# Small fp32 matmuls of three stages regrouped by array tile, and a 16-block inverse packed into 32 columns

## Chip, cores, metric

One core of a Trainium2 chip. The metric is the device time of one execution in microseconds (us), the median of the runs shown. The profile is of one further execution.

## The reference, cut to what matters

The kernel runs two two-layer blocks over 512 tokens of width 1024. The change touches three stages, all in fp32 accuracy.

Memory cross attention, twice (4 heads of 256, 256 memory rows): `p = softmax(q @ k.T / 16)`, `o = p @ v`, `o @ wo`.

Gated linear attention (GLA), once, 4 heads, chunks of 64 tokens: `scores = tril(q_dec @ k_inv.T)`, `o = scores @ v + q_dec @ S`, with `S` updated from chunk to chunk by `k_end.T @ v`, then a norm per head.

The delta rule (RWKV7), once, 8 heads of 64. The reference solves `(I - A_ab) sol = [a_dec, A_ak v]` in chunks of 16; the kernel does the same recurrence in chunks of 64. It inverts the diagonal 16 x 16 blocks of the 64 x 64 lower triangle by the product `(I+A)(I+A^2)(I+A^4)(I+A^8)`, since A^16 is zero there, and brings in what lies off the blocks (`off`) by three further products.

## The kernel before, in words

Every matmul goes through one helper (L190), every ScalarE copy through L207, every VectorE two-operand operation through L213. A dense product splits both sides into a high and a low fp32r part and issues three matmuls; each stands as one row of the trace. A matmul on unsplit fp32 stands as two rows, each with a weight load of its own. Weights come from HBM in units of 256 columns (SP's queue), ScalarE makes the high part (`W.round`), VectorE the low part (`W.rest`), two units ahead. Engines run their own programs in order and wait on semaphores; PSUM has eight banks, which `ps.take` hands out in turn from a list.

**Cross attention** (`xattn`, L996). Per head: scores (L1040), softmax on ScalarE and VectorE, transposes (`turn`), ScalarE's copy of them (`turned`, L1182), and `output_of` (L1063): four fp32 matmuls of 128 x 128 by 512. Query projections and output rows stand between these, in an order written out by hand.

**GLA** (`gla`, L1935). `updates` (L1989) makes the 8 chunk products of two heads, 16 matmuls with 64 x 64 weights: first those on array rows 0 to 63, then those on 64 to 127. `part` does one head's scores (4 matmuls, 64 rows and 128 columns of the array), its output (4 full ones, then 7 from the states, 64 rows and 128 columns), or its norm's sum. `heads()` (L1967) places these parts between sixteen blocks of the memory projection (24 matmuls of 256 columns each), on TensorE, VectorE and ScalarE alike. Those blocks take turns on two banks that ScalarE's copy empties.

**Delta rule** (`rwkv`, L2270). Heads go in four pairs p. Two chains, one for p = 0 and 2, one for p = 1 and 3 and begun 13 rounds later, run in step: each round (`together`, L425) issues the next piece of the one, of the other, and a number of dense pieces from the list `PIECES` (L2312), each three matmuls of a projection or one block of the second memory projection. Per p a chain has 6 rounds of features, 11 of heads and 11 of tail; from one piece to the next of the same chain stand VectorE's masks and sums or ScalarE's copies. The heads' pieces on TensorE (`heads_tensor`, L2408), all with 64 x 64 weights: two Gram products AdT and Ad (`gram`, L2421, 16 matmuls each; first those that stay in their half of the array, then, after a semaphore, those that cross over); aak and arb likewise; Q2T, Q2 and z (`square`, L2434, 16 each); Q4T, Q4, Y1; Q8, Y2; ark with Y3 between its halves; M and MT; then X0 to X2 (`apply`, 128 columns); G and S; and in the tail QT and y. VectorE's part is `heads_vector` (L2658), ScalarE's `heads_scalar` (L2826).

## Time and profile before

| | us |
|---|---|
| median of 3 runs (lowest, highest) | 2987.49 (2987.06, 2989.36) |
| the profiled execution, its own time | 2989.32 |
| its span in the profile | 2987.5 |
| TensorE busy | 2942.3 |
| VectorE, ScalarE, GpSimd busy | 1854.6, 1345.3, 324.1 |

The span is what the trace covers; the execution's own time is 1.8 us longer. GLA lies at about 14 to 183 us, the delta rule at 183 to 505, the first cross attention at 509 to 601, the second at about 1172 to 1263. The trace counts a matmul as busy from its start to its modelled end, so busy times of overlapping matmuls are a union, and a window's (x) counts the rows that run in it, also those begun before.

### The profile page before, as it was taken

To read this page: it belongs to the slowest core of one execution; us is meant where nothing else is said; L and a number is where in the kernel's file an instruction comes from. 1 tells how busy PE (TensorE), PEld (TensorE's weight loads), DVE (VectorE), ACT (ScalarE), POOL (GpSimd) and SP (SyncE) were. 2 spreads that over 40 slices of the span, in tenths; PEclk is the share of its full clock that TensorE was granted. 3 is DMA by queue.
4 is the path that set the end of the run, shared out by engine and by line. 5 is a ranking of instruction groups with operands and counts; after the bars stand their busy time and mean duration, and the time that the engine had idled before them with its cause. 6 is when DMAs were issued, how large, how long until landed. Compare 5 with 4: busy or idle time off the path is not lost.

```text
span 2987.5 us, 43166 instructions
## 1 busy us (share of the span) xinstructions
PE 2942.3 (98%) x18348; PEld 2479.3 (83%) x18348; DVE 1854.6 (62%) x2299; ACT 1345.3 (45%) x1799; POOL 324.1 (11%) x296
## 2 busy tenths in 40 slices
PE   8999999999999999999999999999999999999999
PEld 7877778787888777787888876799988888889998
DVE  5554565367776866367776656766665554566665
ACT  5543444345444674344434447544443333344442
POOL 0010001010000111010000200142410000014240
PEclk9999999999999999999999999999999999999999
DMA  5340123223333223133332331233332222233331
GB/s 193 120 128 16 49 88 127 86 81 93 99 103 96 93 71 113 43 83 105 97 107 93 91 83 29 78 102 103 103 119 77 97 84 79 86 91 103 103 103 67
DMA packets 329120, 275.00 MB, mean 92 GB/s; under 512 B 28784, under 2 KB 286832, under 8 KB 328416
## 3 DMA queue, kind: packets, MB, share of 16 engines
q1 hardware_dynamic: 324560, 252.83, 28.5%
q0 software_dynamic: 4368, 19.41, 1.9%
q8 instruction: 144, 2.36, 0.3%
q14 instruction: 48, 0.39, 0.0%
HBM read 263.83 MB, written 8.39 MB: 91 GB/s over the span
## 4 chain that ended last, share of the span: by engine, by line
PE 88%; DVE 7%; ACT 4%; issue 1%; DMA 0%; DVEq 0%; SPq 0%; ACTq 0%
PE ps L190 87%; DVE arena L213 2%; ACT whi L207 2%; DVE wlo L213 1%; DVE split L213 1%; PE ps L193 1%; ACT arena L207 1%; ACT arena L204 1%; DVE arena L221 1%; ACT split L207 1%; DVE hT L213 0%; DVE xlo L221 0%; DVE sml L230 0%; DVE arena L224 0%; ACT L204 0%
## 5 line engine op out<-in xcount | busy, mean ns | idle before, releaser
L190 PE MATMUL ps<-split,whi 128*128 128x512 f32 (+2 forms) x3296 | 942.6, 364 | 7.0 <-ACT arena L207 4.6
L213 DVE TENSOR_TENSOR wlo<-wraw,whi 128x2048 fp32r<-128x2048 f32 (+3 forms) x262 | 562.2, 2147 | 431.9 <-ACT whi L207 431.1
L190 PE MATMUL ps<-xhi,whi 128*128 128x512 f32 (+1 forms) x1896 | 689.5, 369 | 7.4 <-DVE wlo L213 3.9
L190 PEld LDWEIGHTS ps<-split,whi 128*128 128x128 f32 (+1 forms) x3296 | 594.1, 188 | 121.0 <-issue 17.7
L190 PE MATMUL ps<-xhi,wlo 128*128 128x512 f32 (+1 forms) x1840 | 668.7, 363 | 0.0
L190 PE MATMUL ps<-xlo,whi 128*128 128x512 f32 (+2 forms) x1800 | 657.2, 365 | 0.0
L207 ACT ACTIVATE whi<-wraw 128x2048 fp32r<-128x2048 f32 (+3 forms) x262 | 457.8, 1749 | 351.1 <-PE ps L190 248.1
L190 PE MATMUL ps<-split,wlo 128*128 128x512 f32 (+2 forms) x1648 | 593.1, 360 | 0.0
L190 PEld LDWEIGHTS ps<-xhi,whi 128*128 128x128 f32 x1896 | 353.7, 188 | 75.9 <-issue 8.8
L207 ACT ACTIVATE arena<-ps 128x256 f32<-128x256 f32 (+1 forms) x429 | 204.9, 482 | 442.1 <-PE ps L190 365.4
L190 PEld LDWEIGHTS ps<-xhi,wlo 128*128 128x128 f32 x1840 | 346.6, 188 | 57.9 <-issue 4.3
L190 PEld LDWEIGHTS ps<-xlo,whi 128*128 128x128 f32 (+1 forms) x1800 | 338.6, 188 | 56.4
L190 PEld LDWEIGHTS ps<-split,wlo 128*128 128x128 f32 (+1 forms) x1648 | 310.7, 189 | 48.3 <-issue 5.0
L213 DVE TENSOR_TENSOR hT<-hT,ps 128x512 f32<-128x512 f32 x328 | 225.1, 686 | 147.4 <-PE ps L190 130.4
L207 ACT ACTIVATE split<-arena 128x512 fp32r<-128x512 f32 (+5 forms) x237 | 195.5, 830 | 248.8 <-DVE arena L213 237.8
L213 POOL TENSOR_TENSOR arena<-arena 128x512 f32<-128x512 f32 (+1 forms) x84 | 105.5, 1260 | 1703.0 <-ACT arena L204 1598.6
L190 PE MATMUL ps<-arena 64*64 64x64 f32 (+6 forms) x4102 | 279.9, 255 | 6.8 <-DVE arena L213 2.3
L190 PEld LDWEIGHTS ps<-arena 64*64 64x64 f32 (+3 forms) x4102 | 207.6, 143 | 69.9 <-issue 41.9
L213 DVE TENSOR_TENSOR arena<-arena,ps 128x256 f32<-128x256 f32 (+4 forms) x290 | 134.6, 479 | 203.2 <-PE ps L190 122.1
L213 DVE TENSOR_TENSOR split<-arena,split 128x512 fp32r<-128x512 f32 (+3 forms) x234 | 219.3, 952 | 50.3 <-ACT split L207 47.7
L190 PE MATMUL ps<-split 128*128 128x256 f32 (+2 forms) x1496 | 211.4, 292 | 0.0
L213 DVE TENSOR_TENSOR arena<-arena 128x512 f32<-128x512 f32 (+4 forms) x249 | 173.5, 705 | 55.0 <-ACT arena L204 30.1
(149 smaller groups left out, 2537.7 us busy)
## 6 DMA issues: line engine op xcount, KB each, us to landing
wraw<-in_ffn_w_up SPq DMA_DIRECT2D x128, 512.0 KB, 5.2
wraw<-in_ffn_w_down SPq DMA_DIRECT2D x44, 768.0 KB, 4.4
wraw<-in_odd_w_in SPq DMA_DIRECT2D x24, 1024.0 KB, 5.1
wraw<-in_ffn_w_gate SPq DMA_DIRECT2D x44, 512.0 KB, 3.9
wraw<-in_xattn_wkv SPq DMA_DIRECT2D x16, 1024.0 KB, 5.6
wraw<-in_xattn_wq SPq DMA_DIRECT2D x8, 1024.0 KB, 5.1
wraw<-in_xattn_wo SPq DMA_DIRECT2D x8, 1024.0 KB, 5.1
wraw<-in_ffn_w_down SPq DMA_DIRECT2D x8, 1024.0 KB, 5.0
```

Of the source, the lines that this page charges most:

```text
L190: return self.e.matmul(out, lhsT, rhs, start=start, stop=stop, skip_group_check=True)
L193: return self.e.transpose(out, in_, ident)
L204: return self.e.activation(out, in_, f, bias=bias, scale=scale, accum_out=acc)
L207: return self.e.activation(out, in_, ACT.Copy, scale=scale)
L213: return self.e.tensor_tensor(out, a, b, op)
L221: return self.e.scalar_tensor_tensor(out=out, in0=a, scalar=s, in1=b, op0=op0, op1=op1)
```

## The change

Cross attention: `v` and the transposed weights are split into high and low parts too, and `output_of` issues six fp32r matmuls per bank in place of two fp32 ones. ScalarE gains a copy of 128 x 2048, VectorE its low part, and eight low parts of 128 x 512.

GLA: `updates`, the scores and the states' products of two heads are interleaved matmul by matmul, so that neighbours lie on array rows 0 to 63 and 64 to 127 and in different banks; `heads()` has the parts two heads at a time and in other places.

Delta rule: aak and arb are interleaved so that four neighbouring matmuls lie on the four 64 x 64 quarters of the array; G, S, QT and y become one piece (`between`) in the same way. AdT and Ad are kept only as their diagonal blocks of 32 x 32, as two sets of 8 x 32 columns in one bank (weights of 64 x 32), while the whole Ad is still made for `off` (weights of 64 x 64). Q2T to Y3 become `packed`: 32 matmuls of 32 x 32 by 32 on the four diagonal tiles of the array, in place of 16 of 64 x 64 by 64. VectorE spreads the packed result into Y again with two masked operations ("whole"). `PIECES` has new numbers, of the same sum, and one more small constant is loaded.

```diff
-                            pe.wait_ge(S.A.of("pT", hd, j), ps.empty("o", hd, d))
-                            i_ = pe.mm(b, vv[:, c:c + P], pT[:, j * T:(j + 1) * T], j == 0, j == 1)
+                            pe.wait_ge(S.V.of("v_lo"), S.V.of("pT_lo", hd, j), ps.empty("o", hd, d))
+                            pe.mm(b, vhi[:, c:c + P], pT[j].hi, j == 0, False)
+                            pe.mm(b, vlo[:, c:c + P], pT[j].hi, False, False)
+                            i_ = pe.mm(b, vhi[:, c:c + P], pT[j].lo, False, j == 1)
                         i_.then_inc(*up(S.P, "o", hd, d))
...
+                def turned_low(hd):
+                    for j in range(2):
+                        dve.wait_ge(S.A.of("pT", hd, j), S.P.of("o", hd - 1, 1) if hd else NEVER)
+                        dve.tt(pT[j].lo, ps.ap("turn", hd, j), pT[j].hi.bitcast(F32), ALU.subtract).then_inc(
+                            *up(S.V, "pT_lo", hd, j, frees=("turn", hd, j)))
...
+                dve.wait_ge(S.A.of("v_hi"))
+                dve.tt(vlo, vv, vhi.bitcast(F32), ALU.subtract).then_inc(*up(S.V, "v_lo"))
...
+                act.wait_ge(l_kv.of("x"))
+                act.copy(vhi, vv).then_inc(*up(S.A, "v_hi"))
                 W.round(act, units[2][0])
...
-                return ((("s", 0),), (("s", 1),), (("o", 0),), (("s", 2), ("o", 1)), (("sum", 0),), (("s", 3), ("o", 2)),
-                        (("sum", 1),), (("o", 3),), (("sum", 2),), (("sum", 3),))
+                return ((("s", 0),), (), (("o", 0),), (("s", 1),), (), (), (("sum", 0), ("sum", 1)), (("o", 1),), (("sum", 2), ("sum", 3)), ())
...
-                    for par_ in range(2):
-                        b = ps.take("U", p, par_, of=(2, 3))
-                        pe.wait_ge(S.A.of("keT", p), S.A.of("v", 3), ps.empty("U", p, par_))
...
+                    bs = [ps.take("U", p, par_, of=(2, 3)) for par_ in range(2)]
+                    pe.wait_ge(S.A.of("keT", p), S.A.of("v", 3), *(ps.empty("U", p, par_) for par_ in range(2)))
+                    for n in range(4):
+                        for hp in range(2):
+                            for par_, b in enumerate(bs):
...
+                                if (n, hp) == (3, 1):
+                                    i_.then_inc(*up(S.P, "U", p, par_))
...
+                def part(what, n):
+                    if what == "sum":
+                        b = ps.take("sum", n, of=(4, 5))
+                        pe.wait_ge(S.A.of("square", n), ps.empty("sum", n))
+                        pe.mm(b, ones, sqs[n % 2]).then_inc(*up(S.P, "sum", n))
+                        return
+                    q, k, both = qk[:, n * T:(n + 1) * T], qk[:, (2 + n) * T:(3 + n) * T], (2 * n, 2 * n + 1)
+                    bs = [ps.take(what, hd, of=(4, 5) if what == "s" else (0, 1, 2, 3)) for hd in both]
                     if what == "s":
...
+                        pe.wait_ge(S.V.of("ke", n), *(ps.empty("s", hd) for hd in both))
                         for i in range(4):
...
+                            c = slice(i * P, (i + 1) * P)
+                            for hd, b, hs in zip(both, bs, (slice(0, 64), slice(64, P))):
+                                i_ = pe.mm(b[:, c], k[hs, c], q[hs, c])
+                                if i == 3:
+                                    i_.then_inc(*up(S.P, "s", hd))
+                    else:
+                        for hd, b in zip(both, bs):
+                            pe.wait_ge(S.V.of("pts", hd), ps.empty("o", hd))
+                            for i in range(4):
+                                pe.mm(b[:, i * P:(i + 1) * P], vT[:, i * 512 + hd * P:i * 512 + (hd + 1) * P],
+                                      pts[hd % 2][:, i * P:(i + 1) * P], i == 0, i == 3)
+                        pe.wait_ge(S.V.of("states", n))
                         for c in range(1, 8):
...
+                            for hd, b, hs in zip(both, bs, (slice(0, 64), slice(64, P))):
+                                i_ = pe.mm(b[:, c * 64:(c + 1) * 64], SS[n][hs, c * P:(c + 1) * P],
+                                           q[hs, c * 64:(c + 1) * 64], False, c == 7)
+                                if c == 7:
+                                    i_.then_inc(*up(S.P, "o", hd))
 
                 run(fm_tensor(pe, S, u_qk, X8, norm.made, fresh=norm, sum_at=12, raw=2, halves=True))
...
-            PIECES = (8, 8, 8, 2, 2, 2, 2, 2, 2, 2, 2, 2, 2, 3, 1, 0, 3, 2, 3, 2, 1, 2, 0, 3, 4, 1, 3, 1, 0, 2, 2, 1, 2, 5,
-                      0, 2, 1, 2, 2, 2, 3, 0, 1, 1, 1, 1, 1, 1, 1, 0, 0, 1, 1, 1, 1, 1, 1, 1, 1, 1, 1, 0, 1, 1, 0, 1, 1, 2)
+            PIECES = (8, 8, 8, 2, 2, 4, 1, 1, 2, 2, 2, 3, 2, 1, 2, 0, 4, 4, 2, 0, 0, 2, 0, 4, 4, 1, 3, 0, 1, 2, 2, 1, 2, 5, 0, 3, 0, 2, 1, 2, 4, 0, 1, 1, 1, 1, 1, 1, 0, 1, 0, 1, 1, 1, 1, 2, 1, 1, 1, 0, 1, 0, 1, 1, 1, 1, 1, 1)
...
-                Ad, AdT, Q2, Q2T, off = B["v"], B["ep"], B["a"], B["t1"], B["t2"]
+                Q2, Q2T, off = B["a"], B["t1"], B["t2"]
+                (AdT, Ad), (S2T, S2), S8, Yp = pair(B["ep"]), pair(B["t1"]), B["a"], B["v"]
...
+                def packed(b, at_, lt, rt):
+
+                    for n in range(8):
+                        c = slice(n * 32, n * 32 + 32)
+                        for r in range(0, P, 32):
+                            rows = slice(r, r + 32)
+                            i_ = pe.mm(b[rows, at_ + n * 32:at_ + n * 32 + 32], lt[rows, c], rt[rows, c])
+                    return i_
...
+                def grams(*both):
+
+                    for turned_ in (0, 1):
+                        if turned_:
+                            pe.wait_ge(*(S.P.of(name, "half", p) for name, _, _, _ in both))
+                        for i in range(4):
+                            for hp in range(2):
+                                for n, (name, b, lt, rt) in enumerate(both):
+                                    r = hp ^ n
+                                    e = hp ^ turned_
+                                    c = chunk(2 * i + e)
+                                    i_ = pe.mm(b[HALVES[e], chunk(r * 4 + i)], lt[HALVES[r], c], rt[HALVES[r], c])
+                                    if (i, hp) == (3, 1):
+                                        i_.then_inc(*(up(S.P, name, p) if turned_ else up(S.P, name, "half", p)))
+
                 def square(name, lt, rt, *events):
...
-                gram("AdT", b1, bi, ad, True)
-                gram("Ad", b2, ad, bi, True)
-                gram("AdT", b1, bi, ad, False)
-                gram("Ad", b2, ad, bi, False)
+                for turned_ in (0, 1):
+                    if turned_:
+                        pe.wait_ge(S.P.of("Ad", "half", p))
+                    for i in range(4):
+                        for hp, hs in enumerate(HALVES):
+                            e = hp ^ turned_
+                            c, other = 2 * i + e, 1 - hp
+                            for q in range(0, 64, 32):
+                                t = slice(c * 64 + q, c * 64 + q + 32)
+                                o = (hp * 4 + i) * 32
+                                rows = slice(e * 64 + q, e * 64 + q + 32)
+                                pe.mm(b1[rows, o:o + 32], bi[hs, t], ad[hs, t])
+                                pe.mm(b1[rows, 256 + o:288 + o], ad[hs, t], bi[hs, t])
+                            i_ = pe.mm(b2[HALVES[e], chunk(other * 4 + i)], ad[HALVES[other], chunk(c)],
+                                       bi[HALVES[other], chunk(c)])
+                    i_.then_inc(*(up(S.P, "Ad", p) if turned_ else up(S.P, "Ad", "half", p)))
+                S.P.mark("AdT", p)
                 yield
...
-                gram("aak", b1, ki, ad, True)
-                gram("arb", b2, bi, r, True)
-                gram("aak", b1, ki, ad, False)
-                gram("arb", b2, bi, r, False)
-                yield
-                square("Q2T", Ad, AdT, V("Ad"))
-                square("Q2", AdT, Ad)
+                grams(("aak", b1, ki, ad), ("arb", b2, bi, r))
+                yield
+                b = bank("Q2", V("AdT"))
+                packed(b, 0, Ad, AdT)
...
-                square("Q4T", Q2, Q2T, A("Q2"))
-                square("Q4", Q2T, Q2)
-                square("Y1", Q2, Y, V("Y0"))
-                yield
-                square("Q8", AdT, Ad, A("Q4"))
-                square("Y2", Ad, Y, V("Y1"))
+                b = bank("Q4", A("Q2"))
+                packed(b, 0, S2, S2T)
+                packed(b, 256, S2T, S2).then_inc(*up(S.P, "Q4", p))
+                packed(bank("Y1", V("Y0")), 0, S2, Yp).then_inc(*up(S.P, "Y1", p))
+                yield
+                packed(bank("Q8", A("Q4")), 0, AdT, Ad).then_inc(*up(S.P, "Q8", p))
+                packed(bank("Y2", V("Y1")), 0, Ad, Yp).then_inc(*up(S.P, "Y2", p))
                 yield
                 b = bank("ark")
                 gram("ark", b, ki, r, True)
-                square("Y3", Q2, Y, A("Q8"), V("Y2"))
+                packed(bank("Y3", A("Q8"), V("Y2")), 0, S8, Yp).then_inc(*up(S.P, "Y3", p))
                 gram("ark", b, ki, r, False)
                 yield
-                square("M", off, Y, V("Y3"))
+                square("M", off, Y, V("whole"))
                 square("MT", Y, off)
                 yield
                 apply("X0", Y, A("z"))
...
+                b_s, b_y = ps.take("S", p, of=of_state), ps.take("y", p, of=of_y)
+                pe.wait_ge(ps.empty("S", p), ps.empty("y", p))
...
+                def between(turned_, i, what):
+
+                    for hp, hs in enumerate(HALVES):
+                        first = not turned_ and i == 0
+                        own, other = hp ^ turned_, 1 - (hp ^ turned_)
+                        c, es, kc = 2 * i + other, HALVES[other], slice(i * P + hp * 64, i * P + hp * 64 + 64)
+                        if what == "u" and c < 7:
+                            i_ = pe.mm(b_s[hs, chunk(c)], beT[es, kc], X[es, hp, i, 64:P], first, False)
+                        elif what == "v" and c < 7:
+                            i_ = pe.mm(b_s[hs, chunk(c)], keT[es, kc], vTM[es, kc], False, False)
+                        elif what == "q" and c:
+                            i_ = pe.mm(bq[hs, chunk(c)], X[es, hp, i, 0:64], arb[es, chunk(hp * 4 + i)])
+                        c, es = 2 * i + own, HALVES[own]
+                        if what == "u":
+                            i_ = pe.mm(b_y[hs, chunk(c)], X[es, hp, i, 64:P], arb[es, chunk(hp * 4 + i)], first, False)
+                        elif what == "v":
+                            i_ = pe.mm(b_y[hs, chunk(c)], vTM[es, kc], ark[es, chunk(hp * 4 + i)], False, False)
+                        elif 0 < c < 7:
+                            i_ = pe.mm(bg[hs, chunk(c)], X[es, hp, i, 0:64], beT[es, kc])
...
+                        for what in "uqv":
+                            i_ = between(turned_, i, what)
+                    i_.then_inc(*(up(S.P, "GU", p) if turned_ else up(S.P, "between", "half", p)))
+                S.P.mark("QT", p)
...
-                    dve.tt(Y, Y, ps.ap(name, p), ALU.add).then_inc(*up(S.V, name, p, frees=(name, p)))
+                    dve.tt(Yp, Yp, ps.ap(name, p)[:, 0:256], ALU.add).then_inc(*up(S.V, name, p, frees=(name, p)))
...
-                masked(AdT, "AdT", "c16t", "AdT")
-                masked(Ad, "Ad", "c16", "Ad", frees=False)
+                dve.wait_ge(S.P.of("AdT", p), S.V.own())
+                for n, a in enumerate(pair(AdT)):
+                    dve.tt(chunks(a), chunks(ps.ap("AdT", p)[:, n * 256:n * 256 + 256]),
+                           cm["p16"][:, n * 32:n * 32 + 32].unsqueeze(1).broadcast_to([P, 8, 32]), ALU.mult).then_inc(
+                        *up(S.V, "AdT", p, frees=("AdT", p)))
                 masked(off, "Ad", "coff", "off")
                 yield
...
+                dve.wait_ge(S.V.own(), S.P.of("z", p))
+                for q in range(0, 64, 32):
+                    dve.tt(chunks(Y)[:, :, q:q + 32], chunks(Yp), cm["m32"][:, q:q + 32].unsqueeze(1).broadcast_to([P, 8, 32]),
+                           ALU.mult).then_inc(*up(S.V, "whole", p))
...
-                copied("Q2T", Q2T)
-                copied("Q2", Q2)
...
+                yield
```

## Rows read from the trace of the kernel before

**Rows 1.** The page: span, TensorE's busy time, chain of waits by engine.

```profile
span 2987.5 us, 43166 instructions
...
PE 2942.3 (98%) x18348; PEld 2479.3 (83%) x18348; DVE 1854.6 (62%) x2299; ACT 1345.3 (45%) x1799; POOL 324.1 (11%) x296
...
PE 88%; DVE 7%; ACT 4%; issue 1%; DMA 0%; DVEq 0%; SPq 0%; ACTq 0%
```

**Rows 2.** Windows of four stretches: us from the start, length, busy time and instructions per engine.

```profile
60.00:183.00 123.00, 122.22 (x814) 108.09 (x812) 69.83 (x81) 54.24 (x72) 8.67 (x16) 1.00 0.41 124
...
227.00:257.00 30.00, 30.00 (x602) 25.18 (x603) 9.15 (x12) 7.78 (x11) 0.00 (x0) 1.00 0.08 20
...
257.00:480.00 223.00, 211.41 (x3484) 177.44 (x3480) 124.87 (x189) 89.06 (x127) 7.60 (x14) 0.98 0.21 66
...
509.00:600.00 91.00, 90.58 (x397) 70.92 (x398) 37.46 (x57) 36.14 (x69) 4.49 (x4) 1.00 0.28 93
```

**Rows 3.** Groups of TensorE's matmul rows by shape, 225 to 480 us.

```profile
L190 PE MATMUL ps<-arena 64*64 64x64 f32 x3072 | 98.6, 221 | 2.3 <-DVE arena L210 1.4 <-DVE arena L213 0.9
...
L190 PE MATMUL ps<-arena 64*64 64x128 f32 x384 | 23.5, 272 | 1.3 <-DVE arena L213 1.3
```

**Rows 4.** Windows of five pieces of the delta rule, TensorE alone.

```profile
227.72:229.56 1.84, 1.84 (x65) 1.00 0.01 4
...
234.57:237.52 2.95, 2.95 (x98) 1.00 0.00 0
...
243.64:245.65 2.01, 2.01 (x65) 1.00 0.04 8
...
267.84:270.52 2.68, 2.68 (x80) 1.00 0.02 6
...
300.41:303.24 2.83, 2.83 (x93) 1.00 0.00 0
```

**Rows 5.** Windows of 0.22 and 0.07 us, TensorE; (x) counts matmul rows in flight.

```profile
80.00:80.22 0.22, 0.22 (x7) 1.00 0.00 0
...
80.43:80.65 0.22, 0.22 (x14) 1.00 0.00 0
...
228.30:228.37 0.07, 0.07 (x10) 1.00 0.00 0
...
228.59:228.66 0.07, 0.07 (x16) 1.00 0.00 0
```

**Rows 6.** Windows of three GLA pieces, and of 16 rows of one column.

```profile
79.83:81.36 1.53, 1.53 (x34) 1.00 0.00 0
...
97.56:98.64 1.08, 1.08 (x9) 1.00 0.00 0
...
106.76:108.46 1.70, 1.70 (x15) 1.00 0.22 77
...
520.46:522.16 1.70, 1.70 (x17) 1.00 0.71 260
```

**Rows 7.** Timeline of TensorE at a change of shape: start, length, what.

```profile
97.23 0.28 PE L190 MATMUL ps<-split,wlo 128*128 128x256 f32 x1
97.35 0.28 PE L190 MATMUL ps<-split,whi 128*128 128x256 f32 x1
97.56 1.16 PE L190 MATMUL ps<-arena 64*128 64x128 f32 x8
```

**Rows 8.** Windows of one head's weighted sum and of one query block, cross attention.

```profile
557.35:560.78 3.43, 3.43 (x9) 1.00 0.02 5
...
541.89:547.54 5.65, 5.65 (x27) 1.00 0.10 36
```

**Rows 9.** Groups by shape of VectorE and ScalarE, 225 to 480 us.

```profile
L213 DVE TENSOR_TENSOR arena<-arena,ps 128x512 f32<-128x512 f32 x34 | 23.4, 688 | 35.8 <-PE ps L190 34.5
...
L213 DVE TENSOR_TENSOR wlo<-wraw,whi 128x2048 fp32r<-128x2048 f32 x10 | 22.9, 2291 | 9.7 <-ACT whi L207 9.7
...
L207 ACT ACTIVATE arena<-ps 128x512 f32<-128x512 f32 x63 | 37.4, 598 | 93.8 <-PE ps L190 71.4 <-PE ps L193 22.0
```

More of the change, by code:

```diff
@@ L1007, in xattn @@
             out = add_units("out", [P] * 8, D["xattn_wo"][l])
-            p, pT = al(1024), al(1024)
+            p, pT = al(1024), [als() for _ in range(2)]
+            vhi, vlo = split[:, at[0]:at[0] + 2048], split[:, v_at:v_at + 2048]
+            al(2048)
             mx, sm, rs16 = sml[:, 0:4], sml[:, 4:8], sml[:, 8:12]
@@ L1147, in vector @@
                 maxima(1)
+                turned_low(0)
                 weights(1)
@@ L2223, in part @@
                     if what == "o":
-                        act.wait_ge(S.P.of("o", hd), S.P.of("sum", hd - 2) if hd > 1 else NEVER, S.A.own())
-                        act.act(sqs[hd % 2], ps.ap("o", hd), ACT.Square).then_inc(*up(S.A, "square", hd))
+                        for hd in (2 * hd, 2 * hd + 1):
+                            act.wait_ge(S.P.of("o", hd), S.P.of("sum", hd - 2) if hd > 1 else NEVER, S.A.own())
+                            act.act(sqs[hd % 2], ps.ap("o", hd), ACT.Square).then_inc(*up(S.A, "square", hd))
                     elif what == "sum":
@@ L2491, in heads_tensor @@
                 yield
[L2492 removed]
+                apply("X2", B["ep"], V("X1"), A("MM"))
                 yield
[L2494 to L2516 removed]
@@ L2518, in tail_tensor @@
+                for turned_ in (0, 1):
+                    if turned_:
+                        pe.wait_ge(S.P.of("between", "half", p))
+                    for i in range(4):
+                        for what in "uqv":
+                            i_ = between(turned_, i, what)
+                    i_.then_inc(*(up(S.P, "GU", p) if turned_ else up(S.P, "between", "half", p)))
+                S.P.mark("QT", p)
             def tail_tensor(pe, p):
@@ L2520, in tail_tensor @@
                 QT, TS, GT, y, n1 = B["v"], B["t2"], B["ep"], B["aak"], B["arb"]
-                arb, ark, vTM, X = B["arb"], B["ark"], B["vTM"], by_head(B["X"])
                 state = ps.ap("S", p)
@@ L2530, in tail_tensor @@
                 step(1)
[L2531 to L2553 removed]
+                b2 = ps.ap("y", p)
                 yield
@@ L2659, in heads_vector @@
                 B = sets[p % 2]
-                Ad, AdT, off, diag = B["v"], B["ep"], B["t2"], B["t1"]
+                AdT, off, diag, Yp = B["ep"], B["t2"], B["t1"], B["v"][:, 0:256]
                 Y, arb, ark, X, EL = B["aak"], B["arb"], B["ark"], B["X"], B["EL"]
@@ L2840, in heads_scalar @@
                 yield
-                copied("Q4T", AdT, S.V.of("Y0", p))
-                copied("Q4", Ad)
+                copied("Q4", AdT, S.V.of("Y0", p))
                 yield
-                copied("Q8", Q2, S.P.of("Y1", p))
+                copied("Q8", Q2, n=256)
                 yield
```

111 lines of the change are left out of this document (28 added, 83 removed).

## The prediction

> **What bounds the kernel.** I read the page first. Its chain of waits is TensorE for 88%, and TensorE is busy for 2942.3 of 2987.5 us [rows 1]; a row is thus worth what it takes on TensorE, unless a wait is exposed in its place. Then the windows by stage. In GLA and in cross attention TensorE is never idle for as much as 1 us in 100, while VectorE and ScalarE work for 30 to 57% of the time; in the delta rule it is idle for 11.6 us of the 223 us from 257 to 480, with VectorE at 56% [rows 2]. So time taken off TensorE counts in full in the first two and less in the third. The groups by shape show how much there is: 3072 rows of 64 x 64 weights by 64 columns, busy for 98.6 us together [rows 3]. A fp32 matmul is two rows.
>
> **The price of such a row.** The piece Q2T, Q2, z has 96 rows and takes 2.95 us, Q8 and Y2 have 64 and take 2.01 [rows 4]: 0.94/32 = 29.4 ns a row. As two neighbours run at once, on opposite quarters of the array, one quarter gives a row each 58 ns. Sixteen rows of one column with 128 columns of weights take 1.70 us, 106 ns each [rows 6]: the weight load sets the pace there, and 64 columns of it would be 53. So I take load and matmul of a quarter as one pipeline of 58 ns, and about 30 ns with 32 columns of weights and 32 of data (half of either).
>
> **Four at once.** GLA's updates issue 16 rows on array rows 0 to 63, then 16 on 64 to 127. In a window of 218 ns in the first part 7 rows are in flight, in one of the same length where the second part has begun 14; in the Gram pieces a stretch of 71 ns has 10 rows in flight with one pair of quarters and 16 where a second pair has started behind it [rows 5]. The four quarters thus run side by side, in two banks, without slowing each other. This is the main support of the forecast. What no row shows is four kept up over a whole piece, 32-wide tiles, and how fast TensorE takes in its instructions when they are shorter.
>
> **The sum, delta rule, for each of the four p:**
> - AdT and Ad: 1.84 us before [rows 4]. After, each half has, for each i, on two quarters four small matmuls (two 32-column tiles, 4 rows each, 4 x 30 = 120 ns) and on the other two a whole one (2 x 58 = 117). 8 x 0.12 = 0.96, and as the second half now waits for the first with nothing between, some 0.3: 1.3. Bounds: 1.0 without that wait; 160 rows at the 29.4 ns seen, 4.7.
> - aak and arb: the same 64 rows, 16 a quarter: 0.93 + 0.3 = 1.25, before 1.84 (aak's row is like AdT's).
> - Q2: two packed products of 64 rows, 16 a tile at 30 ns, 0.48 + 0.04 for the start, and z as before (32 x 29.4 = 0.94): 2.1 for 2.95. Bounds of a packed product: 0.48, and 64 x 29.4 = 1.88 where the old square took 0.94. I take the lower end: rows in flight doubled with the quarters.
> - Q4T, Q4, Y1: three packed, 1.6 for 2.95. Q8, Y2: 1.1 for 2.01. ark with Y3: 0.94 + 0.52 and two changes of shape, 1.65 for 1.84.
> - G, S, QT, y: 80 and 92 rows, 2.68 + 2.83 = 5.5 [rows 4]. After, 172 rows over four quarters: 43 x 58 = 2.5 + 0.3 = 2.8.
> - M, MT, MM, X0 to X2, the steps: as before.
>
> Together 18.9 becomes 11.8, 7.1 us less, 28 us for four. VectorE (0.69 us for 128 x 512 [rows 9], an estimated 0.42 for half of it, since 2048 columns take 2.29 and so each further 512 take 0.53) has ten operations of a heads chain turned into four whole and eight half ones, 0.8 us less; ScalarE has five copies of 0.60 turned into two and a half. But the latency of a step stays (a copy of 0.60, or a sum of 0.4 and then for "whole" two of 0.4, and some 0.2 for the semaphore), and its cover shrinks: a dense piece of two units is 1.59 us, and the other chain's piece is now shorter too. Two or three steps in each p with one dense unit or none beside them should show 0.5 us each, 6 us together. Range of that: 0 to 14. I book 22 us.
>
> **GLA.** Updates: 32 rows in 1.53 us, of which a third overlaps already; at four at once 8 x 109 ns (two passes' worth of the 64-column row) and a start, 0.95: 2 x 0.6 = 1.2 less. Scores: 8 rows in 1.08 a head; two heads on separate halves in the same 1.08: 2.1 less. States: 14 rows in 1.70 a head: 3.4 less [rows 6]. Together 6.7. The double sums put some 7 us of ScalarE's and VectorE's work (per head Ln, Exp, copy and two products, each 0.6 to 0.75, and a table load) between two copies that empty the memory blocks' two banks, which come 3.1 us apart; the second pair of squares queues behind that, and so do `W.round` and SP's next load. Up to 3 us; I book 1.2, so 5.5.
>
> **Cross attention.** Per head 8 rows in 3.43 us become 12 of fp32r; a query block of 24 such takes 5.65 [rows 8], so 2.83 at most and 2.72 at their spacing. 0.7 x 8 = 5.6 less. The new work: ScalarE's 1.9 us copy stands ahead of a `W.round`, whose low part then is ready some 2 us later, still 10 us before its block; VectorE's 2.29 us stands beside the exponentials; the low parts (1.4 us a head) fall in the 2.7 to 5.7 us of dense work between the transposes and `output_of`. I cost these at nothing; if the cover of the last head (2.7 us, against 0.6 + 0.7 + 0.7 in a row) fell short it would be 0.5 us, twice. The added constant's DMA lies 10 us ahead of its first use: nothing.
>
> Sum: 22 + 5.5 + 5.5 = 33. The profiled execution took 2989.3 us, so 2956; the median of the runs is 1.8 lower, so 2955.
>
> **Rivals.**
> *Half the gain.* The four tiles run, but the intake of instructions holds them at two pairs' pace: 14.6 ns a row. A packed product then takes 0.93, what the square did, and AdT and Ad 2.6 us. What is left is 0.6 + 2.7 - 0.8 - 0.2, 2.3 us a p, 8 with some wait: 2989.3 - 8 - 11 = 2970. The same is reached if VectorE's chain exposes 20 us rather than 6. For: no longer stretch is faster than 29 ns a row. Against: the bursts [rows 5]. Chance 0.22.
>
> *Changes of shape.* Where the trace goes from 128 x 128 to 64 x 128 the next row starts 0.21 us after the last, where 0.12 is the spacing of its kind [rows 7]: 0.09 us lost. There the new shape takes cells which the old one still uses. In AdT and Ad small and whole tiles alternate 32 times a p, but within a half each quarter keeps one shape; I therefore take no loss. If it is lost nonetheless, each of 16 groups takes 0.12 + 0.12 + 2 x 0.09 us, 6.7 in place of 1.3, 22 us over four: 2978. Chance 0.18.
> The Trainium skill (TensorEngine Tiling, Key Properties) says that changing the tiling mode, not just the tile, drains TensorE. By that rule this rival is the case; rows 7 agree with it, but show it only for overlapping tiles.
>
> *Slower: the intake is the bound.* If TensorE takes a row (load and matmul) no faster than some 25 ns, the new code loses by its count: without X0 to X2 a p has 716 rows before (21.0 us at 29.4) and 1068 after, 26.7 us at 25. The point from which it decides is 21.0/1068 = 20 ns a row. 5.7 x 4 = 23 more, 11 less from the other stages: 3001. For: 29.4 ns is the pace over whole pieces. Against: 16 rows in flight in 71 ns, which such an intake could feed only from a store. Chance 0.16.
> The Trainium skill (TensorE: Matmul & The Clock Gate, "Wait — 56ns, not 53.3ns?") gives a start-to-start floor of about 25 ns for any small matmul; an estimate by that page is this rival. The trace does not settle whether that holds for each tile or for all.
>
> *The change does not do what it says*: the tiles share a bank or a load path and run as pairs, with the new code's waits around them. The packed rows at half size then cancel their number and only cross attention and part of GLA remain: about 2980 to 2988. Chance 0.06.
>
> **How the numbers follow.** My own case has 0.38 (range 2943 to 2966: the 6 us of exposed waits at 0 or 14, and GLA's 3 us). About 0.2%, 6 us, is what a measurement of this kernel can tell from no change, so faster means below 2981.5. The first case and the half gain lie below (0.60), of the change of shape two thirds (0.12): 0.72. Same: 0.12. Slower: 0.16. The range reaches from the best end, 2943, to the slow rival, 3001.
>
> **What would show it.** Right: windows of aak and arb near 1.25 us, of Q4T, Q4, Y1 near 1.6, of `between` near 2.8; GLA's state rows 14 pairs in 1.7; cross attention's output 2.72 a head; TensorE's idle time in the delta rule up by 5 to 10 us. Wrong: packed rows at 25 ns or more apart; AdT and Ad above 4 us with gaps of 0.1 us at each change of width; TensorE waiting for ScalarE in GLA's last memory blocks; waits for VectorE of over 15 us in the delta rule.

## The result: slower, and the profile after

The changed kernel takes 3021.47 us (median of 4 runs, 3021.09 to 3025.86) against 2987.73: a ratio of 1.0116, interval 1.0104 to 1.0129. The forecast was 2955, and 3001 the top of its range: the kernel got 1.2% slower where 1.1% faster was forecast. The profiled execution spans 3019.3 us, 31.8 more than before.

The page after (span, busy time by engine, TensorE's clock by slice):

```profile
span 3019.3 us, 46063 instructions
...
PE 2956.5 (98%) x19788; PEld 2490.3 (82%) x19788; DVE 1863.8 (62%) x2325; ACT 1342.7 (44%) x1793; POOL 322.7 (11%) x297
...
PEclk9998889999999999999999999999999999999999
```

TensorE's busy time went up, by 14 us [rows 1], and the granted clock, at full speed in every slice of the page of before, is now at 8 tenths in three slices, the fourth to the sixth (226 to 453 us). So the first thing to ask is where the stages stand. Single operations of VectorE that both kernels have show it (timeline: start, length, what). Before:

```profile
201.86 0.49 DVE L217 TENSOR_SCALAR arena<-arena,par 128x512 f32<-128x512 f32 x1
...
507.07 2.29 DVE L213 TENSOR_TENSOR wlo<-wraw,whi 128x2048 fp32r<-128x2048 f32 x1 [1.87 <-ACT whi L207]
...
604.72 2.29 DVE L213 TENSOR_TENSOR wlo<-wraw,whi 128x2048 fp32r<-128x2048 f32 x1 [6.14 <-ACT whi L207]
...
1299.40 0.16 DVE L213 TENSOR_TENSOR sml<-par 128x8 f32<-128x8 f32 x1
```

After:

```profile
197.57 0.49 DVE L219 TENSOR_SCALAR arena<-arena,par 128x512 f32<-128x512 f32 x1
...
544.46 2.29 DVE L215 TENSOR_TENSOR wlo<-wraw,whi 128x2048 fp32r<-128x2048 f32 x1 [1.87 <-ACT whi L209]
...
639.18 2.29 DVE L215 TENSOR_TENSOR wlo<-wraw,whi 128x2048 fp32r<-128x2048 f32 x1 [6.13 <-ACT whi L209]
...
1331.13 0.16 DVE L215 TENSOR_TENSOR sml<-par 128x8 f32<-128x8 f32 x1
```

At the start of the delta rule the changed kernel is 4.3 us ahead (0.95 of it already at 17 us, ahead of any edit), at the start of the first cross attention 37.4 behind, 34.5 after it, and 31.7 after the second. GLA gave 3.3 to 4.3 us, the cross attentions 2.9 and 2.7, and the delta rule cost 41.7. One stage of the three carries the whole miss.

Windows of TensorE in that stage (us from the start, length, busy and matmul rows, granted clock): the AdT and Ad piece of the four p, then aak with arb, Q2 with z, Q4T to Y1, Q8 with Y2, ark with Y3, and the joint piece `between` of the first p:

```profile
221.27:231.62 10.35, 10.29 (x162) 0.69 0.02 4
284.99:297.36 12.37, 12.31 (x172) 0.50 0.01 1
357.37:367.80 10.43, 10.37 (x169) 0.71 0.01 2
430.42:442.34 11.92, 11.86 (x200) 0.63 0.01 1
233.13:235.60 2.47, 2.27 (x66) 0.52 0.00 0
237.12:239.48 2.36, 2.36 (x160) 1.00 0.02 7
242.46:245.25 2.79, 2.06 (x194) 1.00 0.00 0
246.76:248.75 1.99, 1.52 (x130) 1.00 0.00 0
250.94:252.95 2.01, 2.01 (x98) 1.00 0.04 8
270.97:274.17 3.20, 3.11 (x173) 1.00 0.02 5
```

AdT and Ad, 1.84 us before [rows 4], take 10.4, 12.4, 10.4 and 11.9: 45.1 in place of 7.4, 37.7 of the 41.7 us. The other pieces gave some time and lost it again in waits and at the lower clock. The four are also where most of the low clock lies. The first piece begins at full clock and loses it on the way. Windows that split it there, one group at either clock, and the stretch just before the second piece:

```profile
221.27:225.25 3.98, 3.98 (x81) 1.00 0.02 6
225.25:231.62 6.37, 6.31 (x83) 0.50 0.01 3
231.62:235.49 3.87, 3.67 (x68) 0.50 0.00 0
222.29:222.80 0.51, 0.51 (x13) 1.00 0.07 16
290.32:291.08 0.76, 0.76 (x11) 0.50 0.00 0
283.28:284.99 1.71, 1.71 (x11) 0.50 0.04 10
```

Half speed (1.2 in place of 2.4 GHz) from 225.25 to 235.49, beginning 4 us into this piece. A group of eight narrow and two whole rows takes 0.51 us at full clock and 0.76 at half: 16 of them are 8.1 or 12.2 us. Within the group at full clock 0.12 us pass from the start of the last narrow row to that of the first whole one, and 0.15 from the last whole row to the next narrow one; the narrow rows start 13 to 18 ns apart. In the third and the fourth piece the clock falls in the same way, 3 to 4.4 us in. The second piece is different: the clock was at half 1.7 us before it began, and in the 2.3 us before that TensorE had been busy for 0.42 only. Over 215 to 510 us the mean clock is 0.88, where it was 0.98, so some 70 us ran at half speed in place of some 12.

The windows of GLA (updates, one pair's scores, one pair's states) and of one head's weighted sum in cross attention, which answer to [rows 6] and [rows 8]:

```profile
78.90:80.00 1.10, 1.10 (x34) 1.00 0.00 0
95.65:96.82 1.17, 1.17 (x18) 1.00 0.00 0
104.49:106.26 1.77, 1.77 (x30) 1.00 0.10 37
594.70:597.42 2.72, 2.72 (x13) 1.00 0.02 6
```

Four quarters at once, and the fp32r matmuls of cross attention, work nearly as forecast (0.95, 1.08, 1.7 and 2.72 were expected). What GLA lost is in its waits (who waited for whom, us in total, times, longest), 14 to 183 us:

```profile
PE ps L192 <- DVE wlo L215: 1.8, 1, 1.8
PE ps L192 <- ACT arena L206: 1.5, 1, 1.5
PE ps L192 <- PE ps L192: 0.8, 1, 0.8
```

4.1 us at the double sums, where I had booked 1.2; before, this stage showed one wait of 1.5.

The group of the packed rows, 215 to 510 us, has the last finding (busy, mean ns of one, idle before them and what ended it):

```profile
L192 PE MATMUL ps<-arena 32*32 32x32 f32 x2048 | 24.1, 201 | 11.0 <-issue 11.0
```

Its first 128, the two products of Q2, start 8.6 ns apart; their window:

```profile
237.12:238.22 1.10, 1.10 (x129) 1.00 0.00 0
```

2048 packed rows are busy for 24.1 us in all, 11.8 ns each, where the rows of the old squares took 29.4. But 11.0 us of idle time stand before them that end with nothing the profile can name ("issue"). Among the waits of TensorE's matmuls in the delta rule of before there is no such line.

### The profile page after: what moved, and what is told of

Read it like the earlier page. It is cut to its first block, busy times and chain, and to the rows that moved or that the text cites. A ratio compares the mean times of both kernels' runs of the same rounds, so it can differ in the third digit from the quotient of the medians.

```text
span 3019.3 us, 46063 instructions
## 1 busy us (share of the span) xinstructions
PE 2956.5 (98%) x19788; PEld 2490.3 (82%) x19788; DVE 1863.8 (62%) x2325; ACT 1342.7 (44%) x1793; POOL 322.7 (11%) x297
## 4 chain that ended last, share of the span: by engine, by line
PE 87%; DVE 7%; ACT 4%; issue 2%; DMA 0%; DVEq 0%; SPq 0%; ACTq 0%
PE ps L192 86%; DVE arena L215 2%; DVE wlo L215 2%; ACT whi L209 2%; PE ps L195 1%; ACT arena L206 1%; DVE split L215 1%; DVE arena L223 1%; ACT arena L209 1%; ACT split L209 1%; DVE hT L215 0%; DVE xlo L223 0%; DVE sml L232 0%; DVE arena L226 0%; ACT L206 0%
## 5 line engine op out<-in xcount | busy, mean ns | idle before, releaser
L192 PEld LDWEIGHTS ps<-split,whi 128*128 128x128 f32 (+1 forms) x3296 | 594.1, 188 | 121.4 <-issue 16.3
L209 ACT ACTIVATE arena<-ps 128x256 f32<-128x256 f32 (+3 forms) x405 | 190.5, 474 | 466.1 <-PE ps L192 411.0
L192 PE MATMUL ps<-arena 64*64 64x64 f32 (+8 forms) x5446 | 267.2, 241 | 20.2 <-issue 14.0
L192 PEld LDWEIGHTS ps<-arena 64*64 64x64 f32 (+5 forms) x5446 | 198.2, 135 | 82.8 <-issue 44.3
L215 DVE TENSOR_TENSOR split<-arena,split 128x512 fp32r<-128x512 f32 (+4 forms) x236 | 222.8, 958 | 53.9 <-ACT split L209 51.4
L192 PE MATMUL ps<-split 128*128 128x256 f32 (+3 forms) x1592 | 234.5, 297 | 0.0
L192 PEld LDWEIGHTS ps<-split 128*128 128x128 f32 x1592 | 214.9, 191 | 8.2 <-issue 0.5
```

The costliest lines, as they stand in the source:

```text
L192: return self.e.matmul(out, lhsT, rhs, start=start, stop=stop, skip_group_check=True)
L209: return self.e.activation(out, in_, ACT.Copy, scale=scale)
L215: return self.e.tensor_tensor(out, a, b, op)
```

## The experiments

**The order within AdT and Ad** (the *reordered kernel* from here on). The same instructions, the narrow ones of a half first:

```diff
                     for i in range(4):
                         for hp, hs in enumerate(HALVES):
...
                                 pe.mm(b1[rows, 256 + o:288 + o], ad[hs, t], bi[hs, t])
+                    for i in range(4):
+                        for hp in range(2):
+                            e = hp ^ turned_
+                            c, other = 2 * i + e, 1 - hp
                             i_ = pe.mm(b2[HALVES[e], chunk(other * 4 + i)], ad[HALVES[other], chunk(c)],
                                        bi[HALVES[other], chunk(c)])
```

> The changed kernel with the AdT and Ad piece in another order, the same instructions: in each half first all the 32-column tiles, then all the 64-column ones, so that the shape changes 3 times a p and not 31 times. Theory A (a change between shapes stops TensorE until all tiles are empty, even where the new tile uses other cells, and the low activity that follows keeps the clock at half): the piece takes 2.5 to 3.6 us in place of 8.1 to 12.2, the half-clock stretches of 10 to 20 us go, and the time is 2980 to 2990. Theory B (the half clock comes from the idle waits of the packed chain, not from this piece): the piece is shorter, but over 40 us at half clock stay, and the time is 3000 or more. Theory C (64-row 32-column tiles are slow in themselves): the piece stays above 6 us, 3010 or more.

Measured: 2985.52 us (2984.13 to 2991.18), ratio to before 0.9995 (0.9986 to 1.0004). The four pieces:

```profile
220.82:224.35 3.53, 3.17 (x162) 1.00 0.01 2
275.42:279.40 3.98, 3.91 (x172) 0.59 0.04 8
337.90:340.90 3.00, 2.93 (x168) 1.00 0.02 5
403.09:406.73 3.64, 3.57 (x172) 0.74 0.02 5
```

14.2 us together for 45.1, and 36 us off the time. Mean clock from 215 to 510 us is 0.95. Theory A holds: it was the alternation that made the piece long, and most of the low clock went with it. B and C fall. About 30 us at half clock stay all the same, the second piece's among them (0.59), and no run tells where these come from.

**The width alone.** The order of the change, but no second shape:

```diff
-                            i_ = pe.mm(b2[HALVES[e], chunk(other * 4 + i)], ad[HALVES[other], chunk(c)],
-                                       bi[HALVES[other], chunk(c)])
+                            for q in range(0, 64, 32):
+                                i_ = pe.mm(b2[e * 64 + q:e * 64 + q + 32, chunk(other * 4 + i)],
+                                           ad[HALVES[other], c * 64 + q:c * 64 + q + 32], bi[HALVES[other], chunk(c)])
```

> The changed kernel with each 64-column matmul of that piece made as two of 32 columns (128 columns of data become two times 64), the order unchanged: no change of width in the piece, 192 more rows in each p... 64 in each half. Theory A (change of shape): a group of 8 and 2 rows that took 0.506 us at full clock becomes 12 rows in 0.12 to 0.25 us, the piece 2 to 4 us, the time 2985 to 2995. Theory C (narrow tiles, or the alternation between the array's row halves, cost by themselves): the group stays at 0.5 us or grows, the piece is 8 us or more, the time 3015 to 3030.

(The count in it is wrong: 16 more matmuls a p, 32 more rows.) Measured: 2988.79 us (2986.25 to 2992.55), ratio 1.0005 (0.9995 to 1.0014). The first piece:

```profile
220.97:224.10 3.13, 2.60 (x194) 1.00 0.01 3
```

3.1 us for 192 rows, 0.47 of it one stretch without any (it ends with "issue" again). A group of 12 rows takes 0.16 us where 10 rows of two shapes took 0.51. With the order left as it was, and the banks taking turns as they did, only the second width made the loss.

**GLA and cross attention alone**, on the kernel before (the hunks of these two stages, nothing else).

> The kernel before with the GLA and the cross attention parts of the change alone. From the two traces GLA is worth 3.4 to 4.3 us and each cross attention 2.9: 2987.7 - 3.9 - 5.8 = 2978. If instead part of these gains came from work that the delta rule of the changed kernel left out (they share queues), it would be 2982 or more.

Measured: 2978.84 us (2977.72 to 2980.02), ratio 0.9969 (0.9957 to 0.9981): 9.1 us, as the two traces had it.

**Siblings together, nothing packed** (the *siblings kernel*). The same, and in the delta rule `grams` for AdT with Ad and for aak with arb, and `between`; the squares, copies and sums of before:

```diff
-                gram("AdT", b1, bi, ad, True)
-                gram("Ad", b2, ad, bi, True)
-                gram("AdT", b1, bi, ad, False)
-                gram("Ad", b2, ad, bi, False)
+                grams(("AdT", b1, bi, ad), ("Ad", b2, ad, bi))
```

> The same kernel (GLA and cross attention parts) with the delta rule's dense products also on all four quarters at once (AdT with Ad, aak with arb, G, S, QT and y together), but nothing packed into 32 columns and the dense pieces placed as before. At the 15.7 ns a row of the changed kernel's joint piece, AdT and Ad take 1.3 us for 1.84, aak and arb the same, the joint piece 3.2 for 5.5: 3.4 us a p, 13.6 in all, and 2978 - 13.6 = 2964. Rival: VectorE's and ScalarE's steps, which stay as they are, set the pace where the dense work is short, and half of it is lost: 2971. Rival: the joint piece asks for the state's and y's banks earlier than before and waits for the other chain's: 2978 or more. The clock stays at full, since no piece mixes shapes.

Measured: 2970.70 us (2969.59 to 2971.62), ratio 0.9943 (0.9928 to 0.9958). 8.1 us for the 13.6 of the sum; the rival that a part is lost to VectorE's and ScalarE's steps had 2971. The stage itself (from the first VectorE operation to the second of the list above, 198.43 to 503.53 us without and 198.03 to 494.40 with the change) shows the split: TensorE's busy time fell by 14.3 us, 288.73 to 274.46, as the sum had it, and its idle time rose by 5.5. Of these, 1.7 are second halves of a piece that wait for the first; the rest lies spread over waits for VectorE, and a little for ScalarE. The reordered kernel is 15 us slower than this one. It differs in what is packed and in the placement of the dense pieces.

**Where the dense pieces stand.** First the reordered kernel with the `PIECES` of before, then the siblings kernel with those of the change (the waits for nothing named are taken up under the next heading).

> The reordered kernel (2985.5) with the dense pieces placed as in the kernel before. If the new placement is what makes room for the packed chain, this is 2988 to 2995; if it is worth nothing or less, 2980 to 2986. The idle time that TensorE spends waiting for nothing the profile shows (17.5 us between 215 and 510) should change by less than 5 us by the theory of code blocks, because the number of instructions is the same.

Measured: 2990.14 us (2984.82 to 2992.43), ratio 1.0006 (0.9997 to 1.0015); the unexplained idle time is 14.8 us, 2.7 less than in the reordered kernel.

> The siblings kernel (2970.7) with the dense pieces placed as in the changed kernel. The placement was found for shorter pieces of the delta rule; I expect 2970 to 2976. If it is the placement and not the packing that costs 15 us in the reordered kernel, this comes out at 2980 or more.

Measured: 2965.12 us (2964.79 to 2966.99), ratio 0.9925 (0.9909 to 0.9942). The new placement is worth 5.6 us on the siblings, more than I thought, and perhaps 4.6 on the packed kernel, whose runs scatter over 7 us. So packing, ordered well, costs 2985.5 - 2965.1 = 20.4 us; by packing I mean all that the two kernels differ in, the narrow AdT and Ad and VectorE's "whole" with it. The delta rule of the two, siblings first:

```profile
197.29:488.16 290.87, 273.19 (x4309) 0.99 0.24 74
197.11:511.83 314.72, 280.77 (x5717) 0.96 0.23 69
```

Of 23.9 us more, 16.3 are idle time of TensorE, and 7.6 are busy time, although each packed product is shorter on its tiles: the packed kernel runs about 25 us of the stage at half clock and the other about 6. So packing loses through the waits first, and then through the clock.

**Code in blocks.** The waits of TensorE's matmuls that end with nothing named, 215 to 510 us, in the changed kernel and in the reordered one:

```profile
PE ps L192 <- issue: 14.0, 11, 2.4
```

```profile
PE ps L192 <- issue: 17.5, 14, 2.4
```

The reordered kernel's timeline of TensorE from 231 us, and its DMA view of 229 to 240 us (the busy share of 40 slices of 0.275 us; the only traffic in it is four transfers of the instruction queue):

```profile
231.65 0.27 PE L192 MATMUL ps<-arena 64*64 64x64 f32 x1 [1.00 <-issue]
231.85 0.50 PE L192 MATMUL ps<-xhi,whi 128*128 128x512 f32 x1
...
233.45 1.22 PE L192 MATMUL ps<-arena 32*32 32x32 f32 x121
235.11 0.83 PE L192 MATMUL ps<-arena 32*32 32x32 f32 x71 [0.43 <-issue]
...
237.47 0.64 PE L192 MATMUL ps<-arena 32*32 32x32 f32 x51
238.84 0.88 PE L192 MATMUL ps<-arena 32*32 32x32 f32 x77 [0.73 <-issue]
```

```profile
DMA  0200000000000200000000000020000000000003
...
q8 instruction: 4, 0.07, 2.7%
```

And the windows from the end of one idle stretch to the end of the next:

```profile
231.65:235.11 3.46, 3.02 (x129) 1.00 0.02 5
235.11:238.84 3.73, 3.00 (x130) 1.00 0.02 4
```

From 231.65 to 235.11 and from there to 238.84 TensorE takes 129 and 130 rows (128 and one in flight at each edge), a load and a matmul each: 256 instructions, which at 16 KB a transfer is one transfer's worth. The transfers stand in slices 2, 14, 27 and 40, so 3.3 to 3.6 us apart to within a slice, the last three each about 1.1 us after the end of an idle stretch. So one block in 3.5 to 3.7 us, 27 to 29 ns a row: that is the pace at which the program arrives here, and packed rows at 8.6 to 9 ns use up a block in 1.1 to 1.2. The same count holds elsewhere: in the changed kernel idle stretches end at 240.69, 244.41 and 247.87 us, again 128 rows apart. The Trainium skill (Runtime: NRT & Kernel Launch, Instruction fetch mechanics) says that an engine's code is refilled in 16 KiB blocks of 256 instructions, and that crossing a boundary is mostly hidden. The block size agrees with this trace; that it is hidden does not, where the instructions are as short as here. Two runs test it, from both sides.

```diff
-                    for n in range(8):
-                        c = slice(n * 32, n * 32 + 32)
+                    for n in range(4):
+                        c = slice(n * 64, n * 64 + 64)
                         for r in range(0, P, 32):
                             rows = slice(r, r + 32)
-                            i_ = pe.mm(b[rows, at_ + n * 32:at_ + n * 32 + 32], lt[rows, c], rt[rows, c])
+                            i_ = pe.mm(b[rows, at_ + n * 64:at_ + n * 64 + 64], lt[rows, n * 64:n * 64 + 32], rt[rows, c])
```

> The reordered kernel with every packed product made of 16 matmuls over 64 columns of data in place of 32 over 32; half of the 32 by 32 weights are left out, so the inverse is not computed. The data that is streamed is the same, TensorE's instructions in the packed products are half: 512 fewer in each p. Theory D (TensorE's program comes in blocks of 16 KB, 256 instructions, and no faster than one block in 3.5 to 3.7 us: the idle stretches that end at 231.65, 235.11 and 238.83 in the reordered kernel are 256 instructions apart): the unexplained idle time falls from 17.5 to under 5 us, and the time from 2985.5 to about 2972. Theory E (the gaps come from the tiles or the banks, which get the same columns): the gaps stay above 12 us, 2980 or more.

Measured: 2962.63 us (2961.74 to 2963.25), ratio 0.9915 (0.9900 to 0.9929); the unexplained idle time:

```profile
PE ps L192 <- issue: 2.1, 4, 1.0
```

17.5 us became 2.1, and the time fell by 22.9, more than the 13 expected. The mean clock from 215 to 510 us is 0.99 again, and half the weight loads are gone too, so this run alone does not say that it was the code. The other does, since it adds instructions and no work, to the siblings kernel with the change's `PIECES`:

```diff
-                        for hs in HALVES:
-                            i_ = pe.mm(b[hs, chunk(n)], lt[hs, chunk(n)], rt[hs, chunk(n)])
+                        for q in range(0, 64, 32):
+                            for hs in HALVES:
+                                i_ = pe.mm(b[hs.start + q:hs.start + q + 32, chunk(n)],
+                                           lt[hs, n * 64 + q:n * 64 + q + 32], rt[hs, chunk(n)])
```

> The siblings kernel with the changed kernel's dense pieces (2965.1), and each matmul of the eleven square products of a p made as two with 32 columns of weights (64 rows of the array, 64 columns of data): the same results, four quarters of half width in place of two whole ones, 176 more matmuls a p (704 more instructions, 2.75 blocks of 256). Theory D (code blocks, one in 3.5 us at the fastest): the unexplained idle time, 0.4 us without this, comes back with 8 to 20 us, and the time is 2972 to 2990 although the tiles have no more to do. Theory E (the idle stretches belong to 32 by 32 tiles or to their banks): none of it, 2960 to 2968.

Measured: 2980.02 us (2978.68 to 2981.00), ratio 0.9974 (0.9964 to 0.9984), 14.9 us slower than without. Its unexplained waits, that line of the same kernel without the doubling, and two windows of the doubled kernel, the first pair of squares and what lies between the ends of two such waits:

```profile
PE ps L190 <- issue: 9.2, 9, 2.1
```

```profile
PE ps L190 <- issue: 0.4, 1, 0.4
```

```profile
226.64:228.63 1.99, 1.99 (x131) 1.00 0.00 0
406.59:410.04 3.45, 1.99 (x128) 1.00 0.02 5
```

The two squares, 128 rows, take 1.99 us, as two squares of 64 rows did [rows 4: Q8 and Y2, 2.01]; nothing grew there but the number of instructions, and 9.2 us of unexplained idle time are in the stage where 0.4 was. The waits end 128 rows and 3.45 us apart here too. Theory D holds; there is no 32 by 32 tile in this kernel, so E falls. The waits are 8.8 of the 14.9 us; TensorE's busy time in the stage also grew by 5.2 us (273.19 to 278.34), of which the clock, 0.98 for 0.99, is a part, and what the rest is was not found.

A long run of short rows does not always wait: from 231.22 us 192 of them run in 2.88 us in the doubled kernel. What counts is how fast the 128 rows of one block pass, dense ones included, and where the block begins.

**GLA's sums one at a time.** In `heads()` the four sums get the slots 4, 6, 8 and 9:

```diff
-                return ((("s", 0),), (), (("o", 0),), (("s", 1),), (), (), (("sum", 0), ("sum", 1)), (("o", 1),), (("sum", 2), ("sum", 3)), ())
+                return ((("s", 0),), (), (("o", 0),), (("s", 1),), (("sum", 0),), (), (("sum", 1),), (("o", 1),), (("sum", 2),),
+                        (("sum", 3),))
```

> The siblings kernel with GLA's four sums of squares each in a slot of its own (slots 4, 6, 8, 9) in place of two and two. TensorE's waits for VectorE's low weight, ScalarE's square and the end of the sums (1.8, 1.5 and 0.8 us in the changed kernel's GLA) should go: 2970.7 - 3.5 = 2967. Rival: the waits move to the output of the second pair, which now comes behind two more slots: 2970 to 2972.

Measured: 2970.63 us (2967.73 to 2970.80), ratio 0.9939 (0.9925 to 0.9954), against 2970.70 without: no gain that can be told. Waits of 1.1, 0.8 and 0.4 us stay in the place of 1.8, 1.5 and 0.8.

> The siblings kernel with the dense pieces of the changed kernel (2965.1) and GLA's four sums in slots of their own. In the siblings kernel the sums alone moved the profiled run by 3 us and the median by nothing. If they add up with the placement: 2962 to 2963; if GLA's wait moves elsewhere, 2965.

Measured: 2963.17 us (2961.90 to 2964.31), ratio 0.9916 (0.9901 to 0.9931); the ranges of the runs with and without the spread sums do not meet, by 0.5 us. This is the fastest kernel that leaves nothing out, 24.7 us below the one before and 58 below the change: siblings together, its placement, the sums spread, and nothing packed.

## Why the prediction was wrong

The runs give the 33.7 us as steps, each a difference of medians. They add up to 33.5; the rest is that the runs of the kernel before that were made with the experiments have a median of 2987.96, and those made with the change 2987.73. The steps at the reordered kernel, whose runs scatter over 7 us, are less certain than the others.

| step | us |
|---|---|
| GLA and cross attention (2988.0 to 2978.8) | -9.1 |
| siblings together in the delta rule (to 2970.7) | -8.1 |
| placement (to 2965.1) | -5.6 |
| packing, shapes kept apart (to 2985.5) | +20.4 |
| shapes alternating in AdT and Ad (to 3021.5) | +36.0 |

*Cross attention*: right, 2.72 us a head and 2.9 and 2.7 us a stage, for 2.72 and 2.8. *GLA*: the pieces are right within 0.15 us; booked 5.5, measured 3.5 (9.1 less 2.9 and 2.7). The term that was mis-sized is the cost of the double sums, booked at 1.2 us, where 4.1 us of waits stand; spreading the sums took 1.8 of them away and gave 2.0 us in the kernel with the new placement, and nothing that can be told in the other.

*Four at once*: right. The joint piece has 172 rows in 3.20 us, where 2.8 was forecast; aak and arb take 1.59 in the reordered kernel for 1.25. The 32 rows of a half start 15 to 16 ns apart, near the 14.5 of the forecast, and the turn between the halves costs more than the 0.3 us a piece that I allowed.

*AdT and Ad: the step that failed.* "within a half each quarter keeps one shape; I therefore take no loss" is wrong. The narrow tiles and the whole one lie in different quarters, and a row of the other width still starts only 0.12 or 0.15 us after the last of the one, where narrow rows follow each other in 0.013 to 0.018 us: 0.27 of the 0.51 us of a group. The Trainium skill (TensorEngine Tiling, Key Properties) says that changing the tiling mode, not just the tile, drains TensorE; rule and trace agree, and the trace adds that it holds where the cells do not overlap. I had this as a rival and gave it 0.18 on the ground of rows 7, which show overlapping tiles only. Its mechanism was right, its price too low: 6.7 us a p was 8.1 at full clock, and what I had not priced at all is the clock. The piece is busy in the records for nearly all of its time, but few rows start in it, and in three of the four the clock fell to half 3 to 4.4 us in; the second ran at half clock from its start. Around the four pieces it stayed there for 10 to 20 us. 8.1 became 12.2, and what followed ran slower too: the three matmuls of the dense unit right behind the first piece start 0.59 and 0.43 us apart, where 0.34 and 0.23 are usual. That the low activity of the piece brought the clock down is inferred from the order in time and from the run that takes the alternation away, where most of it goes; it was not shown by itself, and the second piece speaks for an earlier cause there.

*Packed products*: the pace of the tiles was right, 0.55 us a product for 0.52, and the place where I took it was not what sets the end. The row in flight count [rows 5] showed a burst, and I read it against the intake rival: "16 rows in flight in 71 ns, which such an intake could feed only from a store". There is such a store, and I did not ask how it is filled. A block of 256 instructions is there at once, and when it is used up sooner the next one comes about 3.5 us after it. (The floor of about 25 ns that I cited from the Trainium skill, TensorE: Matmul & The Clock Gate, is none for TensorE as a whole: rows start 8.6 ns apart, 34 ns on each of the four tiles.) The rival's price per row, some 25 ns, was near the 27 to 29 measured, but it binds only where the 128 rows of a block would pass in less than 3.5 us. Kept to that, it cost 17.5 us of idle time in the reordered kernel and 14.0 in the changed one. The 29.4 ns a row of the old squares lies at the same pace, so in the kernel before neither could be seen apart from the other; a packed product takes about half the time on the tiles and doubles the instructions, of which the program was already bringing in nearly as many as it can. Q4 with Y1 shows it: 2.79 us, of which 2.06 busy, for 1.6 forecast; Q8 with Y2 1.99, of which 1.52 busy, for 1.1. (ark with Y3 took 2.01 for 1.65, with no wait in it.) Packing was forecast to save 3.3 us a p, 13 in all; without the waits, in the kernel with half the instructions, the whole program is 2.5 us faster than with no packing.

*VectorE's chain*: booked at 6 us exposed, 0 to 14 in range. Siblings alone lost 5.5 of 13.6, which is about the size that I had booked; it went to many small waits, for VectorE in the main, none of which grew by more than 1.2 us.

The range failed because its slow end was one rival by itself. Here two of them held at once, with a third effect, the clock, on top. The change of shape adds 23 us to the forecast and the intake 46, which would have been 3024 together. That this is near 3021 is luck: the alternation cost 36.0 us, and the rest of the delta rule came out 28.7 above its forecast (20.4 lost by packing and 13.7 gained, for 22 booked), so one price was too low and the other too high.

(Two readings that nothing hangs on: rows 2 show VectorE and ScalarE at 40 to 57% in GLA and cross attention, not 30 to 57; and the shape changes 31 times a p within the piece, not 32.)

## What to carry to other kernels

Order small matmuls by tile shape first and by anything else second, even where their quarters are disjoint; here the alternation took three times the time of one shape, and then the clock. Count TensorE's instructions as well as its tile time: where 256 of them (128 loads and 128 matmuls) would pass, again and again, in less than about 3.5 us, smaller tiles buy little or nothing, and the tile that halves the time should not double the count. Rivals that do not exclude each other belong into the range as a sum.

## What the runs showed that I had not expected

- Alternating between 64 x 64 and 64 x 32 tiles that share no cells takes 0.51 us for ten rows, where twelve rows of one width take 0.16 us.
- Rows on four 32 by 32 tiles start every 8.6 to 9 ns, in bursts of up to 128 rows; the idle stretches after them end 256 instructions apart.
- The instruction transfers of TensorE's queue were nowhere in the delta rule less than 3.2 us apart, in any of these kernels; doubling the instructions of the squares, with equal time on the tiles in the pair that was looked at, cost 14.9 us, 8.8 of them in such waits.
- The granted clock fell to half inside a piece in which TensorE counts as 100% busy (3.98 of 3.98 us up to the fall). Busy time in the records did not foretell the clock here.
- Placement that was made for the packed code gained 5.6 us in code without it.
